# Softmax pipeline of a hybrid attention trunk: a fifth probability tile, transposes and what follows them one slot later

## What is computed

```python
for l in range(DEPTH):                       # 2
    h = rms_norm(x, norm_g[l])
    proj = einsum('btd,dc->btc', h, w_in[l]) # q, k, v, gates, merge columns
    y_a = nsa_mixer(q_a, kv_a, g_a, ...) * silu(z_a)
    y_b = fox_mixer(q_b, k_b, v_b, f_b, b_forget[l]) * silu(z_b)
    merged = sigmoid(r_a) * (y_a @ w_proj_nsa[l]) + sigmoid(r_b) * (y_b @ w_proj_fox[l])
    x = x + merged @ w_out[l]
return rms_norm(x, final_g)
# nsa: compressed attention over 31 blocks, plus selected blocks, plus a window; with 8 blocks and
# top 8, selected and window attention are both causal softmax attention over 512 keys.
# fox: s = q.k * scale + F[q] - F[k], causal softmax, times v.
```

## Time and profile before

| | us |
|---|---|
| median of 3 runs | 1459.05 (1458.85 to 1459.27) |
| the profiled execution, its own time | 1458.66 |
| its span, first to last instruction | 1456.9 |
| PE busy | 1441.6 (99%) |
| PEld busy | 1223.3 (84%) |
| DVE busy | 1030.2 (71%) |
| ACT busy | 906.7 (62%) |
| POOL busy | 491.4 (34%) |

### The profile page before, as it was taken

One profiled execution on the slowest core, in us unless ns is written; L12 is line 12 of the kernel. 1 busy time (PEld: TensorE's weight loads), 2 busy tenths in 40 slices (PEclk: granted clock), 3 DMA queues, 4 the chain that ended last, 5 costly groups with the idle time before them and its releaser, 6 DMA issues.

```text
span 1456.9 us, 22913 instructions
## 1 busy us (share of the span) xinstructions
PE 1441.6 (99%) x7490; PEld 1223.3 (84%) x7490; DVE 1030.2 (71%) x2431; ACT 906.7 (62%) x1912; POOL 491.4 (34%) x578
## 2 busy tenths in 40 slices
PE   9999999999999999999999999999999999999998
PEld 7888888888888888888888888888888888888887
DVE  6837888888888874444576488888888887643444
ACT  6636888778878752223364487788788887522234
POOL 2403664555556420000022155554565555000000
PEclk9999999999999999999999999999999999999999
DMA  9232212212122143333453321212122121433332
GB/s 284 75 101 59 58 47 57 59 45 59 45 59 53 51 130 92 96 101 90 111 184 89 101 53 51 59 44 59 47 57 58 45 58 46 144 92 104 92 101 91
DMA packets 201627, 118.29 MB, mean 81 GB/s; under 512 B 9305, under 2 KB 195889, under 8 KB 201009
## 3 DMA queue, kind: packets, MB, share of 16 engines
q1 hardware_dynamic: 199120, 107.49, 27.1%
q0 software_dynamic: 1728, 8.66, 1.6%
q10 hardware_dynamic: 672, 0.83, 0.2%
HBM read 110.54 MB, written 6.42 MB: 80 GB/s over the span
## 4 chain that ended last, share of the span: by engine, by line
PE 84%; ACT 6%; DVE 4%; issue 4%; POOL 1%; DVEq 0%; POOLq 0%; ACTq 0%
PE acc L1888 54%; PE turned L1962 6%; PE o_pair L1987 6%; PE scores L1945 3%; PE scores L1947 3%; PE turned L2214 2%; ACT q_fox L891 2%; PE scores L2214 1%; ACT prob L963 1%; ACT w_hi L842 1%; PE turned L2138 1%; DVE prob L1447 1%; PE misc L2007 1%; DVE q_fox L1359 1%; PE scores L1888 1%
## 5 line engine op out<-in xcount | busy, mean ns | idle before, releaser
L1888 PE MATMUL acc<-u_lo,w_hi 128*128 128x512 f32 x968 | 380.1, 393 | 0.0
L1888 PE MATMUL acc<-u_hi,w_hi 128*128 128x512 f32 x968 | 379.4, 392 | 0.0
L1888 PE MATMUL acc<-u_hi,w_lo 128*128 128x512 f32 x968 | 378.8, 394 | 0.0
L1272 DVE TENSOR_TENSOR w_lo<-w_raw,w_hi 128x1024 fp32r<-128x1024 f32 x184 | 231.1, 1256 | 126.8 <-ACT w_hi L842 125.8
L963 ACT ACTIVATE prob<-prob,row_max 128x384 f32<-128x384 f32 (+3 forms) x384 | 215.3, 561 | 119.7 <-DVE row_max L1447 113.8
L842 ACT ACTIVATE w_hi<-w_raw 128x1024 fp32r<-128x1024 f32 x184 | 193.4, 1052 | 151.4 <-PE acc L1888 95.3
L765 POOL TENSOR_SCALAR prob<-prob,row_inv,gates 128x256 f32<-128x256 f32 (+3 forms) x256 | 184.0, 720 | 215.1 <-DVE row_inv L1454 214.4
L1888 PEld LDWEIGHTS acc<-u_hi,w_lo 128*128 128x128 f32 x968 | 182.0, 188 | 34.0
L1888 PEld LDWEIGHTS acc<-u_hi,w_hi 128*128 128x128 f32 x968 | 181.8, 188 | 33.5 <-issue 0.2
L1888 PEld LDWEIGHTS acc<-u_lo,w_hi 128*128 128x128 f32 x968 | 181.9, 188 | 32.1 <-issue 0.2
L1447 DVE CUSTOM_DVE_ANT_0 prob<-scores,causal 128x384 f32<-128x384 f32 (+3 forms) x384 | 184.4, 480 | 19.2 <-PE scores L1947 18.2
(11 more groups left out here) (330 smaller groups left out, 2562.9 us busy)
## 6 DMA issues: line engine op xcount, KB each, us to landing
w_raw<-in_w_in_dram SPq DMA_DIRECT2D x140, 512.0 KB, 3.7
w_raw<-in_w_proj_nsa_dram SPq DMA_DIRECT2D x16, 512.0 KB, 3.8
w_raw<-in_w_proj_fox_dram SPq DMA_DIRECT2D x16, 512.0 KB, 3.8
w_raw<-in_w_out_dram SPq DMA_DIRECT2D x16, 512.0 KB, 3.8
x_scratch<-xT POOLq DMA_DIRECT2D x2, 2048.0 KB, 8.7
xT<-x_scratch POOLq DMA_DIRECT2D x2, 2048.0 KB, 8.8
x_nat<-in_x_dram SPq DMA_DIRECT2D x4, 512.0 KB, 6.5
c_w<-in_cmp_w_k_dram SPq DMA_DIRECT2D x4, 512.0 KB, 5.5
```

Source lines behind the costliest of these rows:

```text
L1272: dve.tensor_tensor(w_lo[:, par, :, 0:width], w_raw[:, par, :, 0:width], w_hi[:, par, :, 0:width], ALU.subtract).then_inc(w_lo_done, 1)
L1888: ins = pe.matmul((bank or acc[par])[0:width, :], own_w, rhs, start=(n == 0), stop=(n == 23))
```

## The change

The ring of probability tiles gets a fifth place (`SM_RING` 5; the fifth tile is `v_raw`, which has no other use in a cycle) and the place of a step is now counted over all steps of a layer. The turns of a pair move from the odd slot in which they stood to the even slot after it (lags 4 and 3 in place of 3 and 2). The upper parts go with them. The lower parts move to odd slots (lags 5 and 4), the value products to even slots (6 and 5), their narrow columns likewise (8 and 7). Taking over and gating of the outputs move with these by a slot, mostly. The scores of fox steps 16 and 20 are made in the slot of the turns with which they are interleaved, which is now slot 16 and 20 in place of 15 and 19. `Plan` counts the new places, so the units begin and end about a slot later: unit 0 of a cycle ends in slot 5 in place of 4, and `qk_of(0)`, `qf_round` and `qf_rest` move from slots 5, 6 and 7 to 6, 7 and 8. `cmp_copy` and `cmp_rest` stay in slots 7 and 8. Each last cycle has 29 slots in place of 28. The wait on `kf_first` counts the second copy of the key rounding in place of the first. No operation is added or taken away.

```diff
-SM_RING = 4
+SM_RING = 5
-LAG_SCALE, LAG_TURN, LAG_PT, LAG_PV = 1, 2, 3, 4
-LAG_NARROW = LAG_PV + 2
+LAG_SCALE, LAG_PV = 1, 5
...
-def both(s, lag):
-
-    return (lag + 1, lag) if (s - lag) % 2 else ()
+def turn_lags(s):
+
+    return () if s % 2 else (4, 3)
+
+
+def low_lags(s):
+
+    return (5, 4) if s % 2 else ()
+
+
+def value_lags(s):
+
+    return () if s % 2 else (6, 5)
+
+
+def narrow_lags(s):
+
+    return () if s % 2 else (8, 7)
...
-        for s, cost in ((1, 2.0), (5, 2.0), (10, 1.0), (18, 1.0)):
+        for s, cost in ((1, 2.0), (5, 2.0), (11, 1.0), (19, 1.0)):
...
+        def prob_of(ring):
+
+            return v_raw if ring == SM_RING - 1 else prob[:, ring, :]
...
-                        if h == 0 and rows == own(0):
+                        if h == 0 and rows == other(0):
...
-                    for lag in both(s, LAG_TURN):
+                    for lag in turn_lags(s):
                         if s < plan.slots and s - lag < CYCLE_STEPS and cycle.step(s - lag):
                             hi_step(*cycle.step(s - lag))
...
-                    at(2, lambda: head_output(before, 0))
-                    at(LAG_PV + 2, lambda: head_output(before, 1))
-                at(8 + LAG_PV + 4, lambda: head_output(nsa, 0))
-                at(16 + LAG_PV + 2, lambda: head_output(nsa, 1))
+                    at(3, lambda: head_output(before, 0))
+                    at(7, lambda: head_output(before, 1))
+                at(16, lambda: head_output(nsa, 0))
+                at(23, lambda: head_output(nsa, 1))
...
-                    for lag in both(s, LAG_PT):
+                    for lag in low_lags(s):
                         if step(lag):
                             lo_step(*step(lag))
```

More of the change, by code:

```diff
@@ L227, in bass_trunk @@
         row_inv = sb("row_inv", [P, SM_RING])
-        sb("up_to_2_kb", [P, 32])
+        sb("up_to_2_kb", [P, 29])
         u_hi = sb("u_hi", [P, KT, T], F32R)
@@ L779, in body @@
                     at(10, lambda: gate_output(Pair(False, l, i - 1, cycle.g)))
-                at(CYCLE_STEPS + 1 if cycle.last else 16 + LAG_PV + 3, lambda: gate_output(cycle.nsa))
+                at(CYCLE_STEPS + 1 if cycle.last else 23, lambda: gate_output(cycle.nsa))
                 if cycle.last:
@@ L2022, in cmp_values, with ending @@
                     pe.matmul(o_pair[:, :], vcb[:, nsa.g, h, :], pc_t[:, :], start=False, stop=False)
-                for slot, what in ((1, cmp_scores), (5, cmp_turn), (10, lambda: cmp_values(0)),
-                                   (18, lambda: cmp_values(1))):
+                for slot, what in ((1, cmp_scores), (5, cmp_turn), (11, lambda: cmp_values(0)),
+                                   (19, lambda: cmp_values(1))):
                     extra.setdefault(slot, []).insert(0, what)
-                def ending(s, lag):
-                    for n in (s - each for each in both(s, lag)):
-                        now = cycle.step(n) if n < CYCLE_STEPS else None
+                def ending(s, lags):
+                    for lag in lags:
+                        now = cycle.step(s - lag) if s - lag < CYCLE_STEPS else None
                         if now and now[0].ends(now[1]):
@@ L2050, in body @@
                     narrow = scored and not scored[0].nsa and scored[0].starts(scored[1])
-                    turns = [cycle.step(s - lag) for lag in both(s, LAG_TURN) if s < plan.slots and s - lag < CYCLE_STEPS]
+                    now = cycle.step(s) if s < CYCLE_STEPS else None
+                    begun = now if now and not now[0].nsa and now[0].starts(now[1]) else None
+                    turns = [cycle.step(s - lag) for lag in turn_lags(s) if s < plan.slots and s - lag < CYCLE_STEPS]
                     turns = [step for step in turns if step]
                     for n, step in enumerate(turns):
-                        turn_step(*step, scored=scored if narrow and n == 0 else None, ended=ended_at(s) if n == 0 else None)
+                        turn_step(*step, scored=begun if n == 0 else None, ended=ended_at(s) if n == 0 else None)
                     if not turns and s < plan.slots and ended_at(s):
```

44 lines of the change are left out of this document (22 added, 22 removed).

## The result

The changed kernel takes 1475.47 us (median; 1475.27 to 1475.65) against 1459.05 before (1458.85 to 1459.27): ratio 1.0115, 95% interval 1.0104 to 1.0126. It is 16.4 us slower, where 5.9 were forecast (1465.0, range 1457.0 to 1470.5).

A forecast was written before the change was run, and what follows sets the result against it. PE was taken as the bound, losing 15 us in waits. Middle cycles +8.2, first +1.1 and last -3.4 gave +5.9 on the profiled 1458.66, 1464.6; with 0.4 for the median, 1465.0 us, range 1457.0 to 1470.5.

The forecast's parts named there:

- PE is the bound, and DVE's lower part the releaser: PE busy 1441.6 of 1456.9 us; its waits at turns 6 and 8 end with DVE's lower parts, not POOL's scaling.
- Middle cycles: Twelve cycles: lower part 4 comes 1.1 us later, turn 6 loses 1.39, turns 8 and 9 are freed: +8.2 us.
- Room for 15 us: Over all cycles PE loses 15 us in waits, the most that the change can gain.
- First cycles: Two cycles: turn 6 costs 1.1 us more, turn 19 gives 0.56 back: +0.54 each, twice +1.1.
- Last cycles: Two cycles: turn 6 free (-0.81), turn 14 mostly, turns 19 and 23: 1.7 of 1.95 us gained, twice -3.4.
- signs that the prediction names: Middle cycles: loads idle about 1.6 us at turn 6, none at 8 and 9, 51.6 us long; last cycles: none at 6.
- Turn 14: Last cycles: its wait, 0.47 us, mostly goes, as the key rounding runs two slots ahead of lower part 12.
- POOL is refuted: First rival: POOL's scaling holds the turns, or the added job costs nothing; gain 9.5 (1449.5) to 15 us (1444); chance 0.12.
- half of the chain is taken up: Second rival: DVE starts the chain to lower part 4 earlier, turn 6 loses about 0.9 us; 1458 us; chance 0.14.
- The third: Third rival: turns 8 and 9 stay late (+5 us), or lower part 12 or output bank adds as much; 1470; chance 0.12.
- The slot of slack for the scaling: Every wait on POOL's scaling gets 2.1 us of slack, which removes the 0.5 at turn 19 in four cycles.
- the forecast's linear price of a wait: Loads' idle ahead of a pair of turns, less 0.23 us, is lost on PE; idle inside a pair is lost whole.

The follow-up runs named there:

- three moves: Kernel before with split for unit 3 two slots later (first, middle cycles), reading of unit 0 ahead of it, split for unit 2 three later (last): 1445.66 us.
- The best kernel with it: Changed kernel with splits for units 2 and 3, unit 0's reading, compressed jobs, first split, head outputs and last cycles' key rounding moved: 1452.25 us (0.9957).

## Why the prediction was wrong

- **PE is the bound, and DVE's lower part the releaser:** right. Removing POOL's work left the waits; moving jobs on DVE and ACT moved them.
- **Middle cycles:** right. Turn 6 1.45 lost (forecast 1.39), turns 8 and 9 free, cycles of 51.6 us for 50.9, +8.9 for +8.2 in sum. The chain to lower part 4 took 6.37 us for 6.33, with DVE's rest in it and ACT's copy at nothing, and the loads at turn 6 stood idle for 1.69 us where 1.62 was forecast. What the working does not say is that ACT's queue, with the copy in it, is nearly as late: moving DVE's rest away gives only 0.67 of the 0.89 back, and the copy another 0.35.
- **Room for 15 us:** held; three moves took 12.7 of it back.
- **First cycles:** +0.54 forecast, +1.49 measured. Turn 6 (1.74) and turn 19 (free) came as forecast. The term that is missing is the score pair's 0.68 and the compressed turn's 0.17: the sum followed only the waits that the trace of before had, and this one was new.
- **Last cycles, the step that failed:** "Last: unit 0 now ends in slot 6, so the fox queries are rounded behind upper parts 4 and 5 and turn 6 is free (-0.81)". The first half is true, the second doesn't follow: turn 6 still lost 0.85. Of the signs that the prediction names this is the one that did not come. I took away the job that had held turn 6 and did not write down what else now stood in those slots. The same slot shift that took the fox queries out brought reading, split and output together in slot 7 (before, split and reading were in slot 5 and the output in slot 6). Moving the split out freed turn 6. That a last cycle, with fewer unit products per slot, also leaves the chain less time, was only argued. Turn 14 failed likewise: the key rounding runs one slot ahead of lower part 12 now as before (slot 16 to 17, 15 to 16), not two, and the first head's output, which stayed in slot 16, came ahead of that lower part. With the score pair (1.02) and the output bank (0.58), neither priced, the last cycles went to +2.1 and +2.4 us each where -1.7 was forecast. These 7.9 us are most of the 10.5 that the forecast missed.
- **The rivals:** POOL is refuted (its scaling cut: -2.5 us, from turn 19 and the like). That half of the chain is taken up is refuted by the 6.37 us. The third named the output bank, which costs 0.58 in each last cycle; but turns 8, 9 and 14 of the middle cycles are in time.
- **The shift itself** is worth nothing measurable in the middle cycles once the queues are in order: they lose 0.51 with it and 0.49 without. The best kernel with it is still slower than the best without. The slot of slack for the scaling frees only turn 19.
- **Open:** why the best variant of the changed kernel stays 6.6 us above the other is for the most part located (in each last cycle a score pair 0.44, turns 0.27, 0.47 and 0.28, the output bank 0.46 and the compressed turn 0.39; in each first one 0.5), but no run took these apart.

## What to carry to other kernels

When steps move by a slot and side jobs stay, or the other way round, write down for every stretch between two deadlines what each engine now has in it, the place that a job enters as well as the one it leaves, and do so for the first and last round apart: they have other lengths and other jobs. A job is worth moving if the stretch that it enters has room for it: a 1.2 us job out of a full stretch gave 6 us over twelve rounds, a 2.1 and a 1.4 us job into one cost 43 and more, a slower split and a lower clock included. Do not take the name of a releaser for granted where that engine had finished microseconds earlier.

## What the runs showed of the hardware

The clock of PE fell behind some of the long waits, and the price of the fall was near that of the wait. With the compressed rest alone moved, the score pair of the last cycle waits alike in both layers. PE in layer one, then in layer two:

```profile
494.50 0.28 PE L2005 MATMUL o_pair<-pt_lo,v_pair 128*128 128x256 f32 x1
496.70 0.50 PE L1963 MATMUL scores<-kk_hi,q_nsa 128*128 128x512 f32 x1 [1.92 <-DVE row_max L1465]
...
1220.10 0.28 PE L2005 MATMUL o_pair<-pt_lo,v_pair 128*128 128x256 f32 x1
1222.31 0.68 PE L1963 MATMUL scores<-kk_hi,q_nsa 128*128 128x512 f32 x1 [1.93 <-DVE row_max L1465]
```

The stretches behind them (length, busy time by engine, granted clock):

```profile
496.70:500.00 3.30, 3.30 (x18) 2.87 (x19) 2.80 (x9) 3.22 (x8) 2.60 (x4) 1.00 0.00 0
1222.30:1225.50 3.20, 3.19 (x8) 2.53 (x9) 2.45 (x8) 2.25 (x7) 2.59 (x4) 0.53 0.00 0
```

After one wait the clock stayed at its upper level (2.4 GHz), after the other, equally long, it was at the lower (1.2) for about 3 us; products of 0.39 us took 0.63 and began 0.43 apart for 0.23, some 1.6 us more in all. With both compressed jobs moved, the same wait came in both layers too, and there the clock was 0.50 behind it in layer one and 1.00 in layer two. Where the fox queries were moved, PE stood 3.0 us ahead of turn 8 in each of the twelve middle cycles. In the cycle shown above the clock was 0.50 of full speed in all of the next 5 us:

```profile
300.20:305.30 5.10, 5.10 (x18) 4.55 (x19) 3.55 (x13) 4.34 (x11) 1.98 (x3) 0.50 0.00 0
```

Over the same 5 us it was 0.50 in one other cycle, 0.66 to 0.73 in eight and 1.00 in two. What decides it no run here shows.

So the forecast's linear price of a wait (idle less 0.23) held for the waits of up to 1.7 us that the kernels before and after have, and is too low for some of the longer ones of these variants. Of the 6.8 us that the cycle shown of the fox queries' variant loses, 3.2 are the wait at turn 8; most of the rest is the clock.

The weight split on DVE (L1290) and the gate product on POOL (L748) held each other up, and the one that began later paid. In the middle cycles of the changed kernel the split begins 0.1 us ahead of the product (289.18 and 289.26 in the fourth cycle) and takes 1.23, the product 2.30. With the fox queries moved, the product begins 0.2 us ahead (294.41 and 294.62) and takes 1.29, the split 2.17. It is so in all twelve middle cycles of either trace. The 0.9 us in DVE's row thus come from the product running beside the split. No run moved the product, so its share in the 43 us of that variant stays open.
